# The opening of a three-layer kernel: modulation summed on VectorE in four column blocks, input transposed first

## What is computed

```python
c_act = jax.nn.silu(c)
mod = c_act @ ada_w[l] + ada_b[l]                      # 1024 x 3072 matrix
shift, scale, gate = jnp.split(mod[:, None, :], 3, axis=-1)
u = _rmsnorm(h, norm_g[l]) * (1.0 + scale) + shift
proj = u @ w_in[l]
...
h = h + gate * y
```

## Time and profile before

| | us |
|---|---|
| median of 3 runs | 2947.9 (2944.35 to 2949.33) |
| profiled execution, its own time | 2948.93 |
| profiled execution, its span | 2947.1 |
| opening block, to its last VectorE instruction (span time) | 72.8 |
| first product of job 0, first of job 2 (span time) | 77.06, 100.58 |

### The profile page before, as it was taken

How to read it: one execution, slowest core, us unless ns; L and a number is a source line. 1 busy time by engine, 2 the same in 40 slices (tenths; PEclk the granted TensorE clock), 3 DMA queues, 4 the chain that set the end, 5 groups by cost and what they waited for, 6 DMA issues and landing times. The chain is left out here.

```text
span 2947.1 us, 33950 instructions
## 1 busy us (share of the span) xinstructions
PE 2794.1 (95%) x13352; PEld 2247.0 (76%) x13352; DVE 1988.3 (67%) x2652; ACT 1007.9 (34%) x1486; POOL 680.3 (23%) x350
## 2 busy tenths in 40 slices
PE   7999999999999989899998899999898999999997
PEld 3788888878887768488765577888787788887776
DVE  4699998764625671699976876784466888883044
ACT  2111112242414331512146521574312455553222
POOL 0000000000100011002110101453214766666663
PEclk9999999999999999999999999999999999999999
DMA  6112222224335551011110032100221222215553
GB/s 268 65 50 64 93 78 72 95 90 129 108 107 171 157 170 36 29 65 50 44 54 26 18 131 80 39 22 26 75 110 62 79 86 86 85 66 171 158 163 128
DMA packets 100186, 265.83 MB, mean 90 GB/s; under 512 B 8050, under 2 KB 35058, under 8 KB 97859
## 3 DMA queue, kind: packets, MB, share of 16 engines
q1 hardware_dynamic: 95122, 245.64, 24.9%
q10 hardware_dynamic: 4656, 17.30, 1.5%
q0 software_dynamic: 256, 0.82, 0.1%
HBM read 218.64 MB, written 45.09 MB: 89 GB/s over the span
## 5 line engine op out<-in xcount | busy, mean ns | idle before, releaser
L325 PE MATMUL pair<-u_hi,w_hi 128*128 128x512 f32 x768 | 300.6, 391 | 9.0 <-DVE w_lo L598 8.7
L547 DVE SCALAR_TENSOR_TENSOR conv_acc<-aT,cols,conv_acc 128x1024 f32<-128x1024 f32 x232 | 297.9, 1284 | 6.8
L326 PE MATMUL pair<-u_lo,w_hi 128*128 128x512 f32 x768 | 299.4, 390 | 0.0
L327 PE MATMUL pair<-u_hi,w_lo 128*128 128x512 f32 x768 | 299.3, 390 | 0.0
L909 POOL TENSOR_TENSOR yrT<-yrT,gate_c 128x1024 f32<-128x1024 f32 x8 | 19.0, 2370 | 793.5 <-ACT yrT L802 793.5
L325 PEld LDWEIGHTS pair<-u_hi,w_hi 128*128 128x128 f32 x768 | 144.6, 188 | 40.1 <-DVE w_lo L598 8.9
L1723 DVE TENSOR_SCALAR_CACHE_REDUCE counted<-choice,top_i 128x384 uint8<-128x384 f32 (+2 forms) x192 | 169.2, 942 | 0.0
L327 PEld LDWEIGHTS pair<-u_hi,w_lo 128*128 128x128 f32 x768 | 144.6, 188 | 30.2
L326 PEld LDWEIGHTS pair<-u_lo,w_hi 128*128 128x128 f32 x768 | 144.6, 188 | 30.2 <-issue 0.5
L1508 POOL TENSOR_TENSOR ch_lo<-wt,ch_hi 128x1024 fp32r<-128x1024 f32 x17 | 41.3, 2432 | 537.8 <-ACT ch_hi L1467 537.8
L325 PE MATMUL pair<-h_hi,ch_hi 128*128 128x512 f32 x400 | 159.7, 399 | 4.6 <-DVE h_lo L1342 2.4
(11 more groups left out here) (467 smaller groups left out, 7224.7 us busy)
## 6 DMA issues: line engine op xcount, KB each, us to landing
wt<-in_w_ch SPq DMA_DIRECT2D x60, 512.0 KB, 3.3
wo_raw<-in_w_out SPq DMA_DIRECT2D x48, 512.0 KB, 3.6
wt<-in_w_down SPq DMA_DIRECT2D x44, 512.0 KB, 3.7
g_raw<-g_spill SPq DMA_DIRECT2D x44, 256.0 KB, 4.1
wt<-in_w_up SPq DMA_DIRECT2D x10, 1024.0 KB, 4.9
w_raw<-in_w_up SPq DMA_DIRECT2D x10, 1024.0 KB, 4.9
g_spill<-g_stage SPq DMA_DIRECT2D x40, 256.0 KB, 2.3
ada<-in_ada_w SPq DMA_DIRECT2D x8, 1024.0 KB, 25.3
```

Source lines behind the costliest of these rows:

```text
L325: nc.tensor.matmul(bank, w[0], x[0], start=(first and k == 0), stop=False)
L326: nc.tensor.matmul(bank, w[0], x[1], start=False, stop=False)
L327: return nc.tensor.matmul(bank, w[1], x[0], start=False, stop=(last and k == n_k - 1))
L547: nc.vector.scalar_tensor_tensor(dst, x, w, conv_acc[:], ALU.mult, ALU.add).then_inc(conv_step, 1)
```

## The change

The opening is written anew, as functions `open_sync`, `open_scalar`, `open_vector` and `open_tensor`, and it now takes in jobs 0 and 1.

- Loads. `x` comes in four quarters, two on ScalarE's queue and two on SyncE's. The host sends the shift and scale thirds as four column blocks (`ada_mod`, 2 MB each): block j holds the 256 shift and 256 scale channels of channel tiles 2j and 2j + 1. Block 0, the first two weight tiles and block 1 follow `x`; blocks 2 and 3 lie where `x_sb` was and are issued when the transposes are done.
- Statistics: the squares alternate between ScalarE and VectorE, and each half of `x` is scaled as its root is there.
- Transposes come first, by position tile; ScalarE copies them to `xT`. They are all ahead of any modulation.
- Modulation: VectorE multiplies each of the eight 128x512 pieces of a block by its column of silu(c) and adds it to `ada_sum[j]` (32 instructions in all). Four products with `ones_col` (N = 1) then sum over partitions and leave per-partition columns. The 16 masked reductions and the matrix products of L251 are gone.
- ScalarE applies scale and shift twice per channel tile, once for `u_hi` and once in place in `xT`; VectorE subtracts (`low`).
- Jobs 0 and 1 are multiplied inside the opening, two channel tiles per block j, as `u_lo` arrives.
- The gate third is one 4 MB load at the start of the next block. VectorE sums it in jobs 4 to 11 (`gate_sum`), with one tap fewer in each of those steps; TensorE sums over partitions ahead of job G0 + 2, and VectorE adds the bias at step G0 + 2. The loads of `cosT` and `sinT` move to step 13.

```diff
...
+        junk = at(20, "junk", [P, TT, D])
+        xT = at(149, "xT", [P, KT, S])
+        N_MOD = 4
+        ada_mod = [at(kb, f"ada_mod{j}", [P, KT, HALF]) for j, kb in enumerate((52, 68, 85, 101))]
+        ada_sum = [at(kb, f"ada_sum{j}", [P, HALF]) for j, kb in enumerate((181, 183, 201, 203))]
+        ada_gate = at(85, "ada_gate", [P, KT, D])
+        adab_gate = at(201, "adab_gate", [P, D])
...
+        XT_PAIR = (2, 0, 1)
+        mod_sum = pair[3][:, 0, 0:4 * N_MOD].rearrange("p (j i) -> p j i", i=4)
...
+        def open_sync(sp):
+            def modulation(j):
+                sp.dma_start(ada_mod[j][:], a["ada_mod"][j, :, :].rearrange("p (k c) -> p k c", k=KT))\
+                    .then_inc(ada_in[j], 16)
+            sp.dma_start(cols[:], a["cols"]).then_inc(consts_in, 16)
+            sp.dma_start(ident[:], a["ident"]).then_inc(consts_in, 16)
+            for q in (2, 3):
+                to, src = x_quarter(q)
+                sp.dma_start(to, src).then_inc(x_in[q], 16)
+            modulation(0)
+            first_tiles(sp, a["w_conv"], 0, glu_w)
+            modulation(1)
+            sp.wait_ge(xt_mm, TT)
+            modulation(2)
+            modulation(3)
+            for n in (2, 3):
+                sp.wait_ge(job_lo, n - 1)
+                sp.dma_start(slot_view(wt, n), a["w_conv"][n, :, :]).then_inc(glu_w[n % 2], 16)
+        def open_scalar(act):
...
+            def modulated(k):
+                j, i = divmod(k, 2)
+                act.wait_ge(g1_ok, j + 1)
+                for to, done in ((u_hi[:, k, :], u_hi_ok), (xT[:, k, :], u_raw_ok)):
+                    nc.scalar.activation(to, xT[:, k, :], ACT.Identity, bias=msum[:, j, i:i + 1],
+                                         scale=g1[:, k:k + 1]).then_inc(done, 1)
+            for q in (0, 1):
+                to, src = x_quarter(q)
+                act.dma_start(to, src).then_inc(x_in[q], 16)
+            act.wait_ge(consts_in, 32)
+            nc.scalar.activation(cact[:], col("c"), ACT.Silu).then_inc(cact_ok, 1)
+            for half in range(2):
+                for t in (4 * half, 4 * half + 2):
+                    square(t)
+                deviation(half)
+            for t in range(TT):
+                act.wait_ge(xt_mm, t + 1)
+                nc.scalar.activation(xT[:, :, t * P:(t + 1) * P],
+                                     flat(pair[XT_PAIR[t % 3]]).rearrange("p (k s) -> p k s", s=P),
+                                     ACT.Copy).then_inc(xt_ok, 1)
+            high_part(act, 0)
+            act.wait_ge(xt_ok, TT)
+            modulated(0)
+            high_part(act, 1)
+            for k in range(1, KT):
+                modulated(k)
+            high_part(act, 2)
+        def open_vector(dve):
+            chain = Count(dve, dve1)
+            steps = [0] * N_MOD
...
+            def modulation(j, count):
+                dve.wait_ge(ada_in[j], 16)
+                for k in range(steps[j], steps[j] + count):
+                    x, c, to = ada_mod[j][:, k, :], cact[:, k:k + 1], ada_sum[j][:]
+                    if k == 0:
+                        nc.vector.tensor_scalar(to, x, c, None, ALU.mult).then_inc(ada_step, 1)
+                        continue
+                    dve.wait_ge(ada_step, KT * j + k)
+                    nc.vector.scalar_tensor_tensor(to, x, c, to, ALU.mult, ALU.add).then_inc(ada_step, 1)
+                steps[j] += count
+            def shift_and_scale(j):
+                dve.wait_ge(mod_mm, j + 1)
+                chain.then(nc.vector.tensor_tensor(msum[:, j, :], mod_sum[:, j, :], col("ada_mod_b", 4 * j, 4), ALU.add))
+                nc.vector.scalar_tensor_tensor(g1[:, 2 * j:2 * j + 2], msum[:, j, 2:4], 1.0, col("norm_g", 2 * j, 2), ALU.add,
+                                               ALU.mult).then_inc(g1_ok, 1)
+            def low(k):
+                dve.wait_ge(u_hi_ok, k + 1)
+                dve.wait_ge(u_raw_ok, k + 1)
+                nc.vector.tensor_tensor(u_lo[:, k, :], xT[:, k, :], u_hi[:, k, :].bitcast(F32),
+                                        ALU.subtract).then_inc(u_lo_ok, 1)
...
+            for t in (1, 3, 5):
+                square(t)
+            normalize(0)
+            square(7)
+            normalize(1)
+            dve.wait_ge(consts_in, 32)
+            dve.wait_ge(cact_ok, 1)
+            modulation(0, KT)
+            low_part(dve, 0)
+            shift_and_scale(0)
+            for j in range(N_MOD):
+                for i in range(2):
+                    if j + 1 < N_MOD:
+                        modulation(j + 1, 2)
+                    low(2 * j + i)
+                    if j == i == 0:
+                        low_part(dve, 1)
+                if j + 1 < N_MOD:
+                    modulation(j + 1, KT - 4)
+                    shift_and_scale(j + 1)
+            low_part(dve, 2)
+        def open_tensor(pe):
+            pe.wait_ge(consts_in, 32)
+            for t in range(TT):
+                pe.wait_ge(xn_ok, t + 1)
+                if t >= 3:
+                    pe.wait_ge(xt_ok, t - 2)
                 for k in range(KT):
...
+                last.then_inc(xt_mm, 1)
+            for j in range(N_MOD):
+                pe.wait_ge(ada_step, KT * (j + 1))
+                for i in range(4):
+                    last = nc.tensor.matmul(mod_sum[:, j, i:i + 1], ada_sum[j][:, i * P:(i + 1) * P], ones_col[:],
+                                            start=True, stop=True)
+                last.then_inc(mod_mm, 1)
+                if j + 1 < N_MOD:
+                    for k in (2 * j, 2 * j + 1):
+                        for n in range(2):
+                            tile_step(pe, n, k)
+                    continue
+                for n in range(2):
+                    for k in (2 * j, 2 * j + 1):
+                        tile_step(pe, n, k)
...
+        def high_part(act, n):
+            act.wait_ge(glu_w[n % 2], 16 * (n // 2 + 1))
+            if n >= 2:
+                act.wait_ge(job_mm, n - 1)
+            nc.scalar.activation(slot_view(w_parts[0], n), slot_view(wt, n), ACT.Copy).then_inc(job_hi, 1)
+        def low_part(dve, n):
+            dve.wait_ge(job_hi, n + 1)
+            nc.vector.tensor_tensor(slot_view(w_parts[1], n), slot_view(wt, n),
+                                    slot_view(w_parts[0], n).bitcast(F32), ALU.subtract).then_inc(job_lo, 1)
+        def tile_step(pe, n, k):
+            if k == 0:
+                pe.wait_ge(job_lo, n + 1)
+            pe.wait_ge(u_lo_ok, k + 1)
+            for h in range(2):
+                last = products(pair_of(n)[:, h, :], [w[:, n % 2, k, :] for w in w_parts],
+                                [x[:, k, h * HALF:(h + 1) * HALF] for x in uT], k, KT)
+            if k == KT - 1:
+                last.then_inc(job_mm, 1)
...
         def first_tensor(pe):
-            for n in range(N_JOBS):
+            for n in range(2, N_JOBS):
...
+                if n == G0 + 2:
+                    pe.wait_ge(gate_step, KT)
+                    pe.wait_ge(evac, evacs(G0 - 1))
+                    for h in range(2):
+                        last = nc.tensor.matmul(pair[2][:, h, :], mean_w[:], gate_bc[:, h * HALF:(h + 1) * HALF],
+                                                start=True, stop=True)
+                    last.then_inc(gate_mm, 1)
                 if n == G0 + 8:
                     pe.wait_ge(csum_ok, KT - 1)
-                    pe.wait_ge(evac, evacs(G0 - 1))
+                    pe.wait_ge(gate_set, 1)
...
-            act.dma_start(cosT[:], a["cosT"]).then_inc(trig_in, 16)
-            act.dma_start(sinT[:], a["sinT"]).then_inc(trig_in, 16)
-            high_part(0)
-            high_part(1)
             for n in range(N_JOBS):
+                if n == 13:
+                    act.wait_ge(gate_step, KT)
+                    act.dma_start(cosT[:], a["cosT"]).then_inc(trig_in, 16)
+                    act.dma_start(sinT[:], a["sinT"]).then_inc(trig_in, 16)
...
+                        act.dma_start(adab_gate[:], bcast(a["ada_b"], 2 * D, D)).then_inc(adab_in, 16)
...
-                if n + 2 < N_JOBS:
-                    high_part(n + 2)
+                if 1 <= n < N_JOBS - 2:
+                    high_part(act, n + 2)
...
+            def gate_sum(k):
+                dve.wait_ge(gate_w_in, 16)
+                if k == 0:
+                    nc.vector.tensor_scalar(gate_bc[:], ada_gate[:, k, :], cact[:, k:k + 1], None,
+                                            ALU.mult).then_inc(gate_step, 1)
+                    return
+                dve.wait_ge(gate_step, k)
+                nc.vector.scalar_tensor_tensor(gate_bc[:], ada_gate[:, k, :], cact[:, k:k + 1], gate_bc[:], ALU.mult,
+                                               ALU.add).then_inc(gate_step, 1)
...
-                if n + 2 < N_JOBS:
-                    low_part(n + 2)
+                if 1 <= n < N_JOBS - 2:
+                    low_part(dve, n + 2)
...
+                if 4 <= n < 4 + KT:
```

(36 more changed lines are left out.)

192 lines of the change are left out of this document (44 added, 148 removed).

## The result

The changed kernel takes a median of **2928.6 us** (2926.4 to 2931.7, 4 runs) against 2946.6 (4 runs, 2944.4 to 2949.3) for the kernel before on the same chip: ratio 0.9933 (0.9921 to 0.9944), 18.0 us less. The forecast was 2936.5, 11.4 us less than the median before that it went by (2947.9), with a range of 2927 to 2945. The sign and the mechanism came out, and the time is in the range; the saving was more than half as large again. The profiled execution took 2929.0 us, its span is 2927.2.

What follows compares the result with a forecast made beforehand. TensorE, busy 95% of the span, was taken as the bound from job 0 on, the opening simply added. 2948.9 - 13.6 (opening) + 2 (gate sums) = 2937.3, with the median 1.0 lower put at 2936.5 us; range 2927 to 2945.

Steps and rivals of the forecast that it cites:

- The end one for one: What the opening saves before TensorE's first dense stretch comes off the program's end one for one; 13.6 us gained.
- The head, 37.1 us: Opening up to the first product: 37.1 us, 40 us earlier than before.
- After 13.5, VectorE squares tiles 3 and 5: Statistics in the opening: squares start once x has landed at 13.5 us, at 1.3 us each.
- Eight copies out of PSUM at 1.2 (as `u_raw` was) end at 31: ScalarE's copies of the transposes in the opening: start at 21.3 us, 1.2 each, end at 31.
- The rounds: Opening's chain of four modulation rounds: 24 products, 12 at half clock (8 us), plus 5.3 us, so 13.3 each.
- the two bounds for the products: A round's 24 products in the opening: 5.4 us at full clock, 10.2 at half; 8 taken.
- The end of the opening: Fourth round starts at 77 us, its last products end at 86, job 2 starts at 87 instead of 100.6.
- The gate product: Gate third's sums over partitions, two TensorE products ahead of job G0 + 2: 2 us lost.
- The taps: Eight taps moved to VectorE's idle time in steps G0 + 4 and G0 + 5; `channel_sum` on time by 3.8 us.
- Rival 1: Clock stays full in the opening: rounds 10.7 to 11 us, job 2 at 79, 2928 us; chance 0.14.
- Rivals 2 and 3: 2: half clock before job 2, or x late, 2944 us, 0.14. 3: moved taps late, 2940 to 2941, 0.05.
- Rival 4: VectorE's 128x512 pieces in the opening cost 1.78 us, job 2 at 107, 2956 us, slower; chance 0.04.

Runs made afterwards that it cites:

- Late x: Changed kernel with block 0 of the modulation put ahead of x quarters 2 and 3 on SyncE's queue; 2936.74 us (one run).
- the Identity copies: Changed kernel with ScalarE's eight copies of the transposes as Identity with per-partition scale and bias instead of Copy; 2929.08 us (one run).
- the half sum: Changed kernel with the last four of block 0's eight modulation pieces on VectorE replaced by tiny writes; 2928.37 us (one run).
- warm: Changed kernel plus ten extra 512-column products into an unused PSUM bank behind the sums of blocks 1 to 3; 2926.28 us, repeated 2929.00.

## Why the prediction was right or wrong

- **The end one for one: right.** 18.8 to 19.7 at job 2 less 1.8 is 17.0 to 17.9; the medians give 18.0, 18.5 and 20.3.
- **The head, 37.1 us: wrong by 4.6, the step that failed.** *"After 13.5, VectorE squares tiles 3 and 5"* took the whole of x as the start, though the first scaling needs only tiles 0 to 3, whose last quarter is there at 10.79; the rest of it (13.8) is hidden behind the first half's squares, root and scaling. So the copies start at 18.1 and not 21.3: 3.2 us. *"Eight copies out of PSUM at 1.2 (as `u_raw` was) end at 31"* took the price of another form; `Copy` takes 1.04, 0.92 apart: 7.4 and not 9.7, 2.3 us. Against these 5.5, from the copies' end to the first product it took 7.0 instead of 6.1. VectorE's block 0, forecast as hidden, ends 1.6 us after the copies and holds `w_lo` back by 0.6 (27.02, with `w_hi` ready at 26.45), and ScalarE's two passes take 2.4 and not 2.1: they were priced at 1.05, a row of `w_hi`, and cost 1.23 each, the mirror of the mistake with the copies. 3.2 + 2.3 - 0.9 = 4.6. Late x, the Identity copies and the half sum each moved one of the three: +3.7 (at equal clock), +0.7, -0.8. In the two profiles whose first sums ran slow the head was off by 3.9 and 3.8.
- **The rounds: right.** 12.5, 13.0 and 13.4 against 13.3, 1.0 us less in three. The part beside the products was 5.1 for 5.3, two errors that cancel: the passes 0.3 too cheap, the sums over partitions 0.95 for 1.2. Of the two bounds for the products warm shows the one at full clock (24 products in 5.6 us from 46.01); no block was slow to its end. Half of the products at half clock was close (8, 12, 13, 14 of 24). The Trainium skill's "TensorE: Matmul & The Clock Gate", section "HAM oscillation", has every burst after a long wait start low: by that rule all four blocks do, and the trace agrees, four of four at 0.43 us a product.
- **The end of the opening:** 9.4 us from the last block to job 2, forecast 10: 0.6 less. 4.6 + 1.0 + 0.6 is the 6.2 at job 2.
- **The gate product:** forecast 2, measured 1.8. **The taps:** forecast 3.8 us of slack, 4.50 of idle seen. Nothing waits for the gate load.
- **Rival 1 (clock stays full)** gave nearly the measured time, 2928, for a wrong reason: the clock was 0.74. By the time alone it would have seemed right; job 2 was to be at 79 by it with rounds of 11, and the rounds were 13. Rivals 2 and 3 had their marks in the trace (the clock, L521's 1.8) and failed. Of rival 2 one thing was there: the transposes started slow, 6 in the microsecond from 16 us and 12 in that from 22, but they began 3.3 us ahead of the copies, and in this profile no copy waits. **Rival 4** needed pieces of 1.5 us; they are 0.752. It rested on the price of L3007 with GpSimd at work, and GpSimd is idle here.

## What to carry to other kernels

A serial chain of small steps (sum, broadcast, scale) that leaves TensorE idle is worth dense work laid between its links, even at half clock: 15.8 of the 18.5 us came from that, and only 2.7 from the shorter chain. Price a chain's head from the piece of the transfer that its first consumer needs, and each step from a row of the same function and operand kinds, not of the same size only. A gain measured at the stage's end is to be read again at the program's end: 5 to 7 us won by filler products arrived as 4.7 and 1.3 in one version and as nothing in the other.

## What the hardware showed unexpectedly

ScalarE's price depends on the form: 128x1024 fp32 out of PSUM in 1.038 us as `Copy`, in 1.224 as `Identity` with a scale and bias per partition, with everything else equal. The sums over partitions, four products of one column (eight instructions on TensorE) with a 128x128 fp32 tile as weights, took 0.95 to 1.05 us, and 1.87 at half clock: a step of four columns costs as much as ScalarE's copy of a whole tile. And moving 2 MB of another transfer ahead of x's second half also delayed a quarter that lay on the other queue (10.79 to 14.01 us), though nothing in its own queue changed; the run shows the delay, and not how the two queues share the transfers.
